# Down projection of a two-layer trunk: product order, the bias row, the norm's multiply and the lower joins rearranged

## The reference, cut to what matters

```python
y = jnp.einsum('btf,fd->btd', jax.nn.gelu(g, approximate=False) * u, w_down)   # d_ff = 2816
x = layer_norm(DEEPNORM_ALPHA * x + y, ln2_g, ln2_b)
```

## Time and profile before

| what | value |
|---|---|
| median of 3 runs | 2312.85 us (2310.52 to 2314.06) |
| the profiled execution: its time, its span | 2320.86 us, 2319.1 us |
| PE busy | 2156.8 us, 93% |
| DVE, ACT, POOL busy | 69%, 45%, 38% |
| mean granted clock of TensorE | 0.975 |
| down projection, first matmul to last, layer 0 | about 884 to 1166 us |
| down projection, layer 1 | about 2026 to 2303 us |

### The profile page before, as it was taken

The page is one execution under the profiler, slowest core; times in us unless marked ns, Lnnn a source line. Parts: engine busy times, 40 slices in busy tenths (PEclk is TensorE's granted clock), DMA queues, the critical chain, the costliest instruction groups (busy, mean ns, idle before and its releaser), DMA issues.

```text
span 2319.1 us, 35307 instructions
## 1 busy us (share of the span) xinstructions
PE 2156.8 (93%) x13868; PEld 1937.6 (84%) x13868; DVE 1605.3 (69%) x2064; ACT 1046.3 (45%) x1867; POOL 887.4 (38%) x554
## 2 busy tenths in 40 slices
PE   7999999899999998789899999989999999988996
PEld 7997677899999997678688866769999999966775
DVE  1477767877777777455845687577777777775467
ACT  3226655444434444344522276464443444353543
POOL 1115255554455452121221342445545544333122
PEclk9999999999999999999999999999999999999998
DMA  5312166144554459999662112643455545699985
GB/s 156 84 33 67 34 203 181 61 121 124 141 147 121 132 130 296 257 250 226 162 163 54 48 49 94 171 147 90 113 144 141 129 125 142 165 277 266 251 194 158
DMA packets 258333, 338.93 MB, mean 146 GB/s; under 512 B 40048, under 2 KB 158576, under 8 KB 258096
## 3 DMA queue, kind: packets, MB, share of 16 engines
q1 hardware_dynamic: 223288, 261.70, 35.7%
q0 software_dynamic: 34880, 74.98, 19.0%
HBM read 217.65 MB, written 98.03 MB: 136 GB/s over the span
## 4 chain that ended last, share of the span: by engine, by line
PE 67%; DVE 14%; DMA 7%; ACT 5%; issue 4%; POOL 3%; SPq 0%; ACTq 0%; DVEq 0%; POOLq 0%
PE ps L2626 36%; PE ps L2718 10%; PE ps L2306 10%; PE ps L2565 5%; DMA araw<-a_scr 4%; DMA w<-in_w_down 2%; DVE dl L1914 2%; DVE al L1918 1%; PE ps L2449 1%; PE ps L2369 1%; PE ps L2475 1%; DVE bnst L1665 1%; DVE rzc L1652 1%; PE ps L2464 1%; PE ps L2428 1%
## 5 line engine op out<-in xcount | busy, mean ns | idle before, releaser
L2626 PE MATMUL ps<-bt,bh 128*128 128x272 f32 (+1 forms) x3520 | 591.4, 290 | 18.8 <-DVE bt L1823 9.4
L2626 PEld LDWEIGHTS ps<-bt,bh 128*128 128x128 f32 x3520 | 503.5, 190 | 20.4 <-DVE bt L1823 9.8
L1278 ACT ACTIVATE bh<-wblk 128x512 fp32r<-128x512 f32 x308 | 183.1, 623 | 490.8 <-POOL wblk L979 290.8
L2626 PE MATMUL ps<-bt,bl 128*128 128x272 f32 (+1 forms) x1760 | 369.4, 290 | 0.0
L2718 PE MATMUL ps<-dh,ah 128*128 128x512 f32 x616 | 251.6, 408 | 53.9 <-DVE al L1918 40.8
L2626 PEld LDWEIGHTS ps<-bt,bl 128*128 128x128 f32 x1760 | 278.5, 190 | 0.0
L967 POOL TENSOR_TENSOR bl<-wblk,bh 128x512 fp32r<-128x512 f32 x98 | 160.7, 1641 | 295.2 <-ACT bh L1278 295.2
L1841 DVE TENSOR_TENSOR bl<-wblk,bh 128x512 fp32r<-128x512 f32 x210 | 162.2, 805 | 140.0 <-ACT bh L1278 140.0
L2718 PE MATMUL ps<-dl,ah 128*128 128x512 f32 x616 | 247.3, 401 | 0.0
L2718 PE MATMUL ps<-dh,al 128*128 128x512 f32 x616 | 246.5, 400 | 0.0
L1914 DVE TENSOR_TENSOR dl<-w,dh 128x512 fp32r<-128x512 f32 x154 | 142.8, 928 | 140.7 <-ACT dh L1368 140.4
(11 more groups left out here) (260 smaller groups left out, 4322.4 us busy)
## 6 DMA issues: line engine op xcount, KB each, us to landing
wblk<-in_w_up SPq DMA_DIRECT2D x88, 512.0 KB, 5.9
a_scr<-hg SPq DMA_DIRECT2D x44, 552.0 KB, 3.5
e_scr<-hg POOLq DMA_DIRECT2D x44, 512.0 KB, 5.7
araw<-a_scr SPq DMA_DIRECT2D x66, 256.0 KB, 4.8
w<-in_w_down SPq DMA_DIRECT2D x66, 256.0 KB, 10.1
araw<-e_scr SPq DMA_DIRECT2D x66, 256.0 KB, 6.5
w<-in_w_down POOLq DMA_DIRECT2D x16, 1024.0 KB, 17.2
wrow<-in_w_out SPq DMA_DIRECT2D x48, 256.0 KB, 4.9
```

What stands on the lines that cost most here:

```text
L1278: act.activation(bh[b][:], block_of(f, b), ACT.Copy).then_inc(S["u_hi"], 1)
L2626: e = nc.tensor.matmul(up_half(f, b, n), lhs, rhs[:, c:HW_] if n else rhs[:, 0:c], start=(k == 0 and m == 0), stop=(k == HK - 1 and m == 2))
```

## The change

P_5 becomes the fourth product and P_6 the fifth, and they swap their banks. The bias row is no longer added by transfers: POOL adds it to tile 8 with an instruction; DVE takes its left half in with P_1 (`first_out`, now on DVE), and the difference of its halves, split by ACT and DVE into `dbh` and `dbl`, goes into P_5's sums in PSUM with two matmuls by an identity for each tile. P_1 reaches the upper left by DVE (`first_join`), the upper right by a transfer (R_P1T). P_6 joins the upper right straight from PSUM; P_1 + P_6 + P_7 are summed in `un` (`second`, `third`), and two transfers (R_U3B, R_U3C) add that to the lower halves, behind `gained` on POOL. In the norm of TOP, DVE does (x - mean) * gain2 (`spread`), ACT only scales, and POOL only issues the transfer of gain3. POOL's residual multiplies stand between its transfers now. `first_gains` moves ahead of `act_block(l, 4)` on SP.

```diff
-P_1, P_2, P_3, P_6, P_5, P_7, P_4 = range(NP)
+P_1, P_2, P_3, P_5, P_6, P_7, P_4 = range(NP)
...
-P_BANKS = {P_1: PX, P_2: PY, P_3: PX, P_6: PY, P_5: PX, P_7: PY, P_4: PZ}
-P_SAMP = {P_1: PY[3], P_2: PX[0], P_3: PY[0], P_5: PY[0]}
+P_BANKS = {P_1: PX, P_2: PY, P_3: PX, P_5: PY, P_6: PX, P_7: PY, P_4: PZ}
+P_SAMP = {P_1: PY[3], P_2: PX[0], P_3: PY[0], P_5: PX[0]}
...
-R_8, R_TOP, R_P1, R_BOT, R_U2T, R_U2B, R_U2C, RADDS = 1, 2, 3, 4, 5, 6, 7, 7
+R_P1T, R_U3B, R_U3C, RADDS = 1, 2, 3, 3
+P1_EV = 6
...
+        un = at("un", [P, 4, T], x_off)[:, :, HT:2 * HT]
+        identr = at("identr", [P, P], f_off + 16384, F32R)
+        dbh, dbl = at("dbh", [P, HT], ring_off + 14336, F32R), at("dbl", [P, HT], ring_off + 6144, F32R)
...
                 first_blocks(l, 2, 4, 7)
+                first_gains(l)
                 act_block(l, 4)
                 first_blocks(l, 3, 7, KP)
-                first_gains(l)
...
                 if t == NB:
-                    pool.wait_ge(S["gain_ok"], 2 * (l + 1))
+                    pool.wait_ge(S["gain_ok"], 4 * l + 2)
+                    pool.wait_ge(S["xp"], xp_n(l, NB))
+                    pool.tensor_tensor(rz, rz, gain[1][0:q, :], ALU.add).then_inc(S["xp"], 1)
 
             def residual_add(l, which):
 
                 n = RADDS * l + which
                 after(pool, "radd", 16 * (n - 1))
-                p1s = p1[:]
-                if which == R_8:
-                    pool.wait_ge(S["xp"], xp_n(l, NB) + 1)
-                    out, src = rzd[NB][0:NS, :], gain[1][0:NS, :]
-                elif which in (R_TOP, R_BOT):
-                    out = rz_top if which == R_TOP else rz_bot
-                    pool.wait_ge(S["xp"], xp_n(l, 3 if which == R_TOP else 7) + 1)
-                    out, src = out[:], gain[1][:].unsqueeze(1).to_broadcast([P, 4, D])
-                elif which == R_P1:
-                    pool.wait_ge(S["p1_ev"], 4 * (l + 1))
-                    out, src = rz_top[:, :, 0:HT], p1s
-                else:
-                    pool.wait_ge(S["joins"], JOINS * l + J_U2 + 4)
-                    if which == R_U2T:
-                        pool.wait_ge(S["joins"], JOINS * l + J_P3 + 4)
-                        out = rz_top[:, :, HT:D]
-                    else:
-                        out = rz_bot[:, :, HT:D] if which == R_U2B else rz_bot[:, :, 0:HT]
-                    src = p1s
+                if which == R_P1T:
+                    pool.wait_ge(S["p1_ev"], P1_EV * l + 4)
+                    pool.wait_ge(S["xp"], xp_n(l, 3) + 1)
+                    out, src = rz_top[:, :, HT:D], p1[:]
+                else:
+                    pool.wait_ge(S["joins"], JOINS * l + J_U3 + 4)
+                    out, src = rz_bot[:, :, HT:D] if which == R_U3B else rz_bot[:, :, 0:HT], un
                 pool.dma_start(out, src, accum_op=ALU.add).then_inc(S["radd"], 16)
 
...
-                pool.wait_ge(S["n_ym"], n + 1)
+                if t not in TOP:
+                    pool.tensor_tensor(rz, rz, gain[2][0:q, :], ALU.mult).then_inc(S["n_ym"], 1)
+                    pool.wait_ge(S["n_ym"], l + 1)
                 after(pool, "n_yp", 16 * n)
...
                 residual(l, NB)
-                residual_add(l, R_8)
                 act_add(l, KP - 2, 2)
                 act_add(l, KP - 1, 0)
-                for t in range(4):
-                    residual(l, t)
+                residual(l, 0)
                 act_add(l, KP - 1, 1)
-                residual_add(l, R_TOP)
+                residual(l, 1)
                 weight_add(l, T_1, 0)
+                residual(l, 2)
                 act_add(l, KP - 1, 2)
-                residual_add(l, R_P1)
+                residual(l, 3)
                 weight_add(l, T_1, 1)
+                residual_add(l, R_P1T)
                 weight_add(l, T_1, 2)
-                for t in range(4, NB):
-                    residual(l, t)
-                residual_add(l, R_BOT)
-                for which in (T_2, T_3, T_4):
-                    for g in range(len(KGRP)):
-                        weight_add(l, which, g)
-                for which in (R_U2T, R_U2B, R_U2C):
-                    residual_add(l, which)
+                for g in range(len(KGRP)):
+                    weight_add(l, T_2, g)
+                    residual(l, 4 + g)
+                weight_add(l, T_3, 0)
+                residual(l, 7)
+                weight_add(l, T_3, 1)
+                weight_add(l, T_3, 2)
+                for g in range(len(KGRP)):
+                    weight_add(l, T_4, g)
                 for t in TOP:
                     gained(l, t)
+                residual_add(l, R_U3B)
...
@@ -1170,8 +1169,8 @@
 
             def x_hi(l, t):
                 act.wait_ge(S["x_tr"], x_n(l, t) + 1)
-                if l and t == 0:
-                    act.wait_ge(S["radd"], 16 * RADDS * l)
+                if l and t in (0, 4):
+                    act.wait_ge(S["radd"], 16 * (RADDS * (l - 1) + (R_U3C if t else R_P1T)))
...
                     act.activation(gain[n][:], gain[n][:], ACT.Copy, scale=ALPHA).then_inc(S["gain_ok"], 1)
-
-            def first_out(l):
-                for i in range(4):
-                    act.wait_ge(S["d_tile"], 4 * (l * NP + P_1) + i + 1)
-                    act.activation(p1[:, i, :], ps[:, PX[i], :], ACT.Copy).then_inc(S["p1_ev"], 1)
+                act.activation(identr[:], ident[:], ACT.Copy).then_inc(S["gain_ok"], 1)
+
+            def row_hi(l):
+                act.wait_ge(S["p1_ev"], P1_EV * l + 5)
+                act.activation(dbh[:], gain[1][:, HT:D], ACT.Copy).then_inc(S["gain_ok"], 1)
 
             def deviation2(l, t):
...
-                act.activation(rzd[t][0:q, :], rzd[t][0:q, :], ACT.Identity, scale=rst2[0:q, t, :], bias=nmr2[0:q, t, :]).then_inc(S["ln_z"], 1)
+                act.wait_ge(S["ln_rs"], ln2_n(l, t) + 1)
+                bias = zero2[0:q, 0:1] if t in TOP else nmr2[0:q, t, :]
+                act.activation(rzd[t][0:q, :], rzd[t][0:q, :], ACT.Identity, scale=rst2[0:q, t, :], bias=bias).then_inc(S["ln_z"], 1)
...
-                        first_out(l)
+                    elif s == 16:
+                        row_hi(l)
                     elif s in (12, 15):
...
                         weight_neg(l, T_4, (41, 42, 44).index(s))
-                    elif 58 <= s < 63:
-                        if s < 62:
+                    elif 58 <= s < 65:
+                        if s >= 60:
+                            normal2(l, TOP[s - 60])
+                        if s < 63:
                             deviation2(l, TOP[s - 58])
-                        if s == 61:
-                            deviation2(l, NB)
...
             def x_lo(l, t):
+                if l and t == 0:
+                    dve.wait_ge(S["joins"], JOINS * (l - 1) + J_U2 + 4)
...
+            def first_out(l, i):
+
+                dve.wait_ge(S["d_tile"], 4 * (l * NP + P_1) + i + 1)
+                dve.tensor_tensor(p1[:, i, :], ps[:, PX[i], :], gain[1][:, 0:HT], ALU.add).then_inc(S["p1_ev"], 1)
...
+            def row_step(l):
+
+                dve.tensor_tensor(gain[1][:, HT:D], gain[1][:, HT:D], gain[1][:, 0:HT], ALU.subtract).then_inc(S["p1_ev"], 1)
+
+            def row_lo(l):
+
+                dve.wait_ge(S["gain_ok"], 4 * (l + 1))
+                dve.tensor_tensor(dbl[:], gain[1][:, HT:D], dbh[:].bitcast(F32), ALU.subtract).then_inc(S["p1_ev"], 1)
+
+            def first_join(l, i):
+
+                dve.wait_ge(S["p1_ev"], P1_EV * l + i + 1)
+                dve.wait_ge(S["xp"], xp_n(l, i) + 1)
+                rz = half_of(i, 0)
+                dve.tensor_tensor(rz, rz, p1[:, i, :], ALU.add).then_inc(S["joins"], 1)
...
                 p, t, half = {J_C11: (P_2, i, 0), J_P3: (P_3, i, 1), J_VT: (P_5, i, 1), J_VB: (P_5, 4 + i, 1),
-                              J_C22: (P_7, 4 + i, 1), J_P7: (P_7, 4 + i, 0), J_C21: (P_4, 4 + i, 0)}[j]
+                              J_P6: (P_6, i, 1), J_C21: (P_4, 4 + i, 0)}[j]
                 dve.wait_ge(S["d_tile"], 4 * (l * NP + p) + i + 1)
-                if j in (J_C22, J_C21):
-                    dve.wait_ge(S["joins"], JOINS * l + {J_C22: J_VB, J_C21: J_P7}[j] + i + 1)
-                else:
-                    dve.wait_ge(S["radd"], 16 * (RADDS * l + {J_C11: R_P1, J_P3: R_TOP, J_VT: R_U2T, J_VB: R_U2B, J_P7: R_U2C}[j]))
+                if j in (J_C11, J_VT, J_P6):
+                    dve.wait_ge(S["joins"], JOINS * l + {J_C11: J_P1, J_VT: J_P3, J_P6: J_VT}[j] + i + 1)
+                elif j == J_VB:
+                    dve.wait_ge(S["xp"], xp_n(l, t) + 1)
+                else:
+                    dve.wait_ge(S["radd"], 16 * (RADDS * l + {J_P3: R_P1T, J_C21: R_U3C}[j]))
                 rz = half_of(t, half)
                 dve.tensor_tensor(rz, rz, ps[:, P_BANKS[p][i], :], ALU.subtract if j == J_P3 else ALU.add).then_inc(S["joins"], 1)
 
             def second(l, i):
 
                 dve.wait_ge(S["d_tile"], 4 * (l * NP + P_6) + i + 1)
```

(97 more changed lines are left out.)

22 lines of the change are left out of this document (13 added, 9 removed).

## The result

The changed kernel's median is 2283.68 us (4 runs, 2282.78 to 2291.83) beside 2313.2 us for the kernel before on the same chip: a ratio of 0.9882, 95% interval 0.9858 to 0.9906, 29.5 us faster. 2263 was forecast, with 2242 to 2282 as the range. The direction is right, the gain is 20 us short, and the time is 1.7 us outside the range.

A forecast was written before the change was run, and what follows sets the result against it. TensorE (PE), busy 93% of the span, sets the time. The terms sum to 26.0 us won in layer 0 and 23.9 in layer 1, together 50: 2312.85 - 50 = 2263 us, range 2242 to 2282.

The forecast's parts named there:

- (a): End of the first product: POOL's four multiplies, set apart, no longer stall PE; 8.1 and 8.8 us won, bounds 4 to 9.
- (b): Second product: 2 MB less on POOL's queue shortens the wait for activation blocks; 6 us won in each layer.
- Rival 1: Second product stays starved of transfers: 1.5 us won there instead of 6, 2272 us in all; chance 0.22.
- rival 2: Bandwidth counts: 9.9 us won in the second product, no loss at the layer's end, 2246 us; chance 0.21.
- (c): Third and fourth products: R_BOT gone, T_2 due eleven steps later; 8.1 and 8.3 us won, bounds 5 and 9.
- (d): Sixth product: no POOL norm multiply or bias, ACT's normalising two steps behind `spread`; 8.6 us won each, bounds 6 and 9.6.
- (e): Identity matmuls: 8 on PE's path with nothing to hide them, costing 1.8 us a layer.
- (f): Layer's end: R_U3B and R_U3C land late behind serialised `gained` transfers; 3 us lost in layer 0, 6 in layer 1.
- Rival 3: Layer's end: lower sums arrive far too late, from 23.5 us a transfer on; slower, 2327 us; chance 0.04.

The follow-up runs named there:

- each alone: Changed kernel, each POOL residual instruction waiting for DVE's split of a given step, the waiting activation addition moved behind the four multiplies; 2268.2 us, ratio 0.9787 to before.
- on DVE: Changed kernel, with POOL's residual instructions for tile 8 and tiles 0 to 3 given to DVE; 2265.71 us, ratio 0.9778 to the kernel before.
- tile 8 by transfer: Changed kernel, with tile 8's bias added by the small transfer of before instead of a POOL instruction; 2282.99 us, ratio 0.9842 to the kernel before.

## Why the prediction was wrong

**The step that failed is (a)**: "The four multiplies get a transfer or a wait between them. One alone holds DVE about 2.6 us ... Tile 8 gets two instructions in a row ..., 4.8 us." That one alone costs nothing is right (each alone), and so is it that a wait parts two of them. That a transfer does is not: its issue, without a wait of POOL's, does not part them, so tile 8's two instructions and tile 0's multiply held one `al` for 7.37 us, against a lead of 4.4, and PE lost 7.3 and 7.7 us at steps 8 and 9. I won 1.5 us a layer instead of 8.5, 14 of the 19 us that are missing. Two further mistakes are in the same step: I placed the multiplies by POOL's program order and not by what each wait in front of them does to their times (in two of the runs a waiting `act_add` pushed them together), and I hid `first_out` and the sample parts in DVE's free time without asking what is late when DVE comes out of a hold: the sample parts, for step 11, 4.1 and 3.1 us.

**(b)** The size was right in layer 0, 2.6 us short in layer 1. The cause given is right for the kernel before, as the run with late stores shows. That `conv_rows` "still stands on SP before the critical block" I named, without a price; its issue took 12.6 and 14.5 us, beside 9.5 before. Of what is left in layer 0's second product 5.3 us are (a)'s, at steps 11 and 12. Rival 1 (starved as before) is out, rival 2's 9.9 was passed only where POOL no longer held DVE for long (36.0 on DVE and 35.7 each alone, 12.2 and 12.5 won): part of what was left in this product hung on POOL's multiplies, by the late sample parts of steps 11 and 12 and, as it seems, by when POOL's transfers go out.

**(c)** The stalls are gone as forecast, 1.9 us short in all: 36.6, and 35.5 without the identity, against 34.9. No run undoes this part alone, so the cause given is argued, not shown.

**(d)** The size was about right (10.1 and 9.5 against 8.6), in layer 1 mostly for the reason that got half a sentence ("ACT stands in order behind DVE's norm bias") and only by a third for the one that I led with, the held `dl`. The 1 us that PE was to wait did not come: step 55 to 65 of layer 1 at 2.7 to 2.8.

**(e)** Exact: step 35 takes 5.0 instead of 3.2 us.

**(f)** The mechanism was right, the serialised transfers, and the place I watched least was the one that cost: the statistics at step 71, "due 17 to 21, wanted 15.5". R_U3B lasted 13.6 us instead of 9.7, and they waited until 24.8 after step 66's start. In layer 0 I missed a way altogether: the same transfers slow the stores that POOL's next work waits for, 3 to 5 us between the layers. PE waiting at step 73 or 74 was one of my signs of being wrong, and it came. Rival 3's transfers of 23.5 us did not.

**The range.** Its upper end does not follow from its own words: rival 1's 2272 with (a) at 4 and (c) at 5 in both layers is 15.3 us more, 2287 and not 2282. That would have taken in the measured 2283.68, but by luck, since (a) won 1.5 us a layer, far under its low bound of 4.

Not tried: whether the transfers of gain3, issued without waiting for each other, would have freed the queue in time.

## What to carry to other kernels

Look at what stands between two GpSimd instructions: here a DMA issue without a wait did not part them for VectorE, and a wait of 0.3 us did. To spread them over the steps takes a gate on VectorE's own progress, and only works if nothing that waits long stands ahead of it in the queue. Before pricing a removed instruction, ask which engine's program order queued behind it: in layer 1 moving the waiting instruction one step back was worth more than removing the work. When a late transfer is awaited in two places, moving the first wait only pays at the second.

## What the runs showed of the hardware

- A VectorE `tensor_tensor` with two SBUF inputs of 0.68 us lasted 7.37, 10.57 and 11.81 us across two, three and four GpSimd instructions with one or two DMA issues and no wait of GpSimd between them (32 of 32 such pairs over all traces); with a wait of 0.29 us or more it was let in between (89 of 89). A DMA issue alone holds nothing: in "each alone" splits of 0.68 us ran beside four issues in a row (941.8 to 946.7). What is held while an issue stands between two instructions the traces don't show.
- Eighteen 4 KB stores took 6.2 us to issue on SyncE's queue at step 40 and 6.4 to 14.5 us at step 18. How full the DMA engines were did not decide it (6.4 us at a share of 1.10 in "on DVE", 12.6 at 1.05 in the changed kernel); it rose, not strictly, with the share of GpSimd's queue: 6.4 us at 52%, 8.0 at 72% ("each alone"), 6.7 at 75% ("tile 8 by transfer"), 9.5 at 80% (before), 12.6 at 88% and 14.5 at 91%.
- An adding transfer of 1 MB landed in 9.7 us before and in 13.6 us beside the transfers of gain3 and the blocks of the last product.
